# Latent attention's input projection: from plain fp32 matmuls to three products of rounded halves

## What is computed

```python
hx = rms_norm(x, norm_g[i]) * (1 + scx) + sx
hc = rms_norm(ctx, norm_g[i]) * (1 + scc) + sc
# mla_mixer(hc, hx, ...)
def project(h, rotate):
    cq, ckv, kr, gate = split_last(h @ w_in, (MLA_Q_RANK, MLA_KV_RANK, MLA_ROPE, MLA_WIDTH))  # 384, 256, 32, 1024
    q = (rms_norm(cq, q_norm_g) @ w_uq) ...
    kv = (rms_norm(ckv, kv_norm_g) @ w_ukv) ...
```

## Time and profile before

| | us |
|---|---|
| device time, median of 3 runs | 1794.86 (1794.18 to 1795.97) |
| the profiled execution, device time | 1794.53 |
| its span, first to last instruction | 1792.7 |
| PE busy in the span | 1705.8 (95%) |
| DVE busy | 1286.5 (72%) |
| ACT busy | 749.0 (42%) |

### The profile page before, as it was taken

How to read it: one execution, slowest core, us unless ns; L and a number is a source line. 1 busy time by engine, 2 the same in 40 slices (tenths; PEclk the granted TensorE clock), 3 DMA queues, 4 the chain that set the end, 5 groups by cost and what they waited for, 6 DMA issues and landing times. The chain is left out here.

```text
span 1792.7 us, 30064 instructions
## 1 busy us (share of the span) xinstructions
PE 1705.8 (95%) x12816; PEld 1491.0 (83%) x12816; DVE 1286.5 (72%) x1938; ACT 749.0 (42%) x974; POOL 6.3 (0%) x14
## 2 busy tenths in 40 slices
PE   2999989999999999998899999999999999999998
PEld 2999979877999989998898789999754556747898
DVE  7876887855877778997877567987552778566744
ACT  2433375333633373434652255342432445334354
POOL 0000000000000000000000000000000000000000
PEclk9999999999999999999999999999999999999999
DMA  9877536443577738883455336776152010251102
GB/s 390 346 280 281 209 118 225 144 187 118 207 289 273 313 118 338 315 308 120 157 209 193 137 141 253 279 279 227 61 203 84 1 47 1 109 231 48 48 25 94
DMA packets 48804, 331.87 MB, mean 185 GB/s; under 512 B 5256, under 2 KB 8480, under 8 KB 9376
## 3 DMA queue, kind: packets, MB, share of 16 engines
q1 hardware_dynamic: 47808, 326.79, 47.8%
q0 software_dynamic: 864, 3.17, 0.7%
HBM read 328.87 MB, written 1.07 MB: 184 GB/s over the span
## 5 line engine op out<-in xcount | busy, mean ns | idle before, releaser
L343 PE MATMUL ps<-xhi,low 128*128 128x256 f32 x2048 | 499.3, 283 | 4.4 <-ACT xhi L1407 4.2
L343 PEld LDWEIGHTS ps<-xhi,low 128*128 128x128 f32 x2048 | 360.5, 191 | 7.0 <-ACT xhi L1407 5.8
L343 PE MATMUL ps<-xhi,whi_wk 128*128 128x256 f32 x1072 | 298.0, 288 | 39.9 <-ACT xhi L1407 38.8
L343 PE MATMUL ps<-xlo,whi_wk 128*128 128x256 f32 x1072 | 290.7, 280 | 0.0
L1407 ACT ACTIVATE wk<-ps 128x256 f32<-128x256 f32 (+5 forms) x219 | 108.2, 502 | 432.5 <-PE ps L343 367.0
L343 PE MATMUL ps<-xa,ring 128*128 128x256 f32 (+1 forms) x1056 | 281.1, 424 | 5.2 <-DVE xa L1989 3.1
L1407 ACT ACTIVATE whi_wk<-ring 128x2048 fp32r<-128x2048 f32 x100 | 191.6, 1919 | 188.3 <-DMA ring<-in_stream_dram 138.1
L343 PEld LDWEIGHTS ps<-xa,ring 128*128 128x128 f32 x1056 | 197.6, 190 | 82.5 <-issue 51.4
L343 PEld LDWEIGHTS ps<-xhi,whi_wk 128*128 128x128 f32 x1072 | 202.8, 194 | 42.8 <-issue 41.2
L1986 DVE TENSOR_TENSOR low<-ring,whi_wk 128x2048 fp32r<-128x2048 f32 (+1 forms) x101 | 228.4, 2264 | 6.6 <-ACT whi_wk L1407 6.6
L343 PE MATMUL ps<-wk 64*64 64x64 f32 (+10 forms) x2712 | 210.3, 262 | 5.9 <-ACT wk L1407 4.3
(11 more groups left out here) (131 smaller groups left out, 2553.4 us busy)
## 6 DMA issues: line engine op xcount, KB each, us to landing
ring<-in_stream_dram SPq DMA_DIRECT2D x302, 1024.0 KB, 5.6
ring<-in_cond_dram SPq DMA_DIRECT2D x4, 1024.0 KB, 4.7
wk<-spread_dram POOLq DMA_DIRECT2D x4, 384.0 KB, 5.4
wk<-spread_dram POOLq DMA_DIRECT2D x2, 768.0 KB, 7.3
tab<-in_tab_dram SPq DMA_DIRECT2D x1, 1440.0 KB, 20.5
res<-in_xt_dram SPq DMA_DIRECT2D x1, 1024.0 KB, 17.5
res<-in_ct_dram SPq DMA_DIRECT2D x1, 1024.0 KB, 9.8
out_dram<-wk SPq DMA_DIRECT2D x4, 256.0 KB, 2.5
```

What stands on the lines that cost most here:

```text
L343: last[0] = nc.tensor.matmul(o, l, r, start=start, stop=stop, skip_group_check=free)
```

## The change

The seven `mla_in` chunks are taken with `take_both`, so that each has a high and a low half, made by ACT (`mla_high`) and DVE (`mla_low`): chunk 0 beside `w13` 20 of the feed-forward, chunks 1 and 2 at the head of `norm(5)`, chunk 3 after the third rank's copy, 4 between the two sums of the ranks, 5 and 6 after gate units 7 and 9. The modulated context and tokens go rounded into `whi_xa` (the memory of `xa`), and their low parts into `x2lo`, which needs the full value beside it: eight more ACT instructions for the context (`xf6`), eight more DVE instructions for the tokens (into `x2f`), and four subtractions on DVE. Each matmul over k becomes three in fp32r. For the context, units 0 to 3 run with the high half alone before `ms2`, 4 and 5 after it, and then all six get their third product. The late modulation chunks start only at chunk 2. `cq_sq` moves to column 4096, since `x2lo` takes its place, and the copy of the rotated key (`k_rope`) stands behind the first logarithm of the ranks.

```diff
+        x2lo = nc.alloc_sbuf_tensor_at("x2lo", [P, KT, 2 * T], F32R, offset=wk_at + 4 * NEW)
...
-        LATE_AT = (0, 1, 2, 3, 4, 5, 6)
+        LATE_AT = {2: (0,), 3: (1, 2), 4: (3, 4), 5: (5,)}
```

PE, in `mla`:

```diff
+                def input_halves(i):
+                    no = take_both("mla_in", i)
+                    eng.wait_ge(vector_done, step("mlow", i))
+                    return tiles(low[:, (no + 1) % RING, :], 256), tiles(low[:, no % RING, :], 256)
+                def with_high(n, both, cs):
+                    (hi, lo), at = both, slice(P * (n % 2), P * (n % 2) + P)
+                    o = bank(n % 6, cs.start, cs.stop)
                     for k in range(KT):
...
+                        if n == 0:
+                            eng.wait_ge(scalar_done, step("xc6" if cs == CS else "xx6", k))
+                        mm(o, hi[:, k, at], whi_xa[:, k, cs], k == 0, False, free=True)
+                        mm(o, lo[:, k, at], whi_xa[:, k, cs], False, False, free=True)
+                def with_low(n, both, cs):
+                    hi, at = both[0], slice(P * (n % 2), P * (n % 2) + P)
+                    for k in range(KT):
+                        if n == 0:
+                            eng.wait_ge(vector_done, step("xlc6" if cs == CS else "xlx6", k // 4))
+                        mm(bank(n % 6, cs.start, cs.stop), hi[:, k, at], x2lo[:, k, cs], False, k == KT - 1, free=True)
+                def unit(n, both):
+                    (hi, lo), at = both, slice(P * (n % 2), P * (n % 2) + P)
+                    for k in range(KT):
+                        mm(bank(n % 6), hi[:, k, at], whi_xa[:, k, :], k == 0, False)
+                        mm(bank(n % 6), lo[:, k, at], whi_xa[:, k, :], False, False)
+                        mm(bank(n % 6), hi[:, k, at], x2lo[:, k, :], False, k == KT - 1)
```

ACT, in `norm` and `mla` (and `mla_high(0)` in `ffn`):

```diff
+            def mla_high(i):
+                n = found["chunk_no", "mla_in", i][1]
+                eng.wait_ge(landed[n % RING], loads(n))
+                eng.wait_ge(*step_of("chunk", n + 1 - RING))
+                act(low[:, (n + 1) % RING, :], ring[:, n % RING, :], ACT.Copy, "mround", i).then_inc(scalar_done, 1)
...
                 if m == 5:
+                    mla_high(1)
+                    mla_high(2)
                     one_table()
...
+                    if m == 5 and kind == "w13" and j == 20:
+                        mla_high(0)
...
+                for t in range(KT):
+                    act(x3[:, t, CS], x3[:, t, CS], ACT.Identity, "xf6", t, scale=x[:, t, 1:2], bias=md[:, t, 1:2]).then_inc(scalar_done, 1)
                 eng.wait_ge(tensor_done, step("ms2", m))
...
+                    if n == 2:
+                        mla_high(3)
                 for i in range(2):
                     eng.wait_ge(tensor_done, step("cqsum", i))
                     log_mean(rs2[:, 512 * i:512 * i + 512], bank(6), (384, 256)[i], EPS, "cqe", i)
+                    if i == 0:
+                        mla_high(4)
+                        eng.wait_ge(vector_done, step("kr"))
+                        act(k_h[64:96, :, :], over(k_rot[64:96, :], 8), ACT.Copy, "k_rope").then_inc(scalar_done, 1)
                 root(rs2, "cqr", m)
                 for n in range(6, 14):
                     gate_out(n)
+                    if n in (7, 9):
+                        mla_high(5 + (n - 7) // 2)
```

DVE, in `norm` for m = 5 (ahead of the wait for `accb` 0), with `mla_low(0)` after `w13` 20 in `ffn`:

```diff
+                else:
+                    mla_low(1)
+                    mla_low(2)
```

DVE, in `mla`:

```diff
+                for i, hs in enumerate(halves):
+                    eng.wait_ge(scalar_done, step("xf6", 4 * i + 3))
+                    tt(x2lo[:, hs, CS], x3[:, hs, CS], whi_xa[:, hs, CS].bitcast(F32), SUB, "xlc6", i).then_inc(vector_done, 1)
                 eng.wait_ge(scalar_done, step("rs2", m))
                 for t in range(KT):
                     tt(x3[:, t, XS], res[:, t, XS], rs2[:, 256:512], MUL, "xn6", t).then_inc(vector_done, 1)
...
+                for t in range(KT):
+                    ts(x2f[:, t], x3[:, t, XS], x[:, t, 0:1], MUL, md[:, t, 0:1], ADD).then_inc(vector_done, 1)
...
+                for i, hs in enumerate(halves):
+                    eng.wait_ge(scalar_done, step("xx6", 4 * i + 3))
+                    tt(x2lo[:, hs, XS], x2f[:, hs], whi_xa[:, hs, XS].bitcast(F32), SUB, "xlx6", i).then_inc(vector_done, 1)
+                mod_part(*LATE_MODS[0])
+                mla_low(3)
                 eng.wait_ge(tensor_done, step("in2", m, 5))
...
+                mod_part(*LATE_MODS[1])
+                mla_low(4)
+                mod_part(*LATE_MODS[2])
                 eng.wait_ge(scalar_done, step("cqr", m))
...
+                mla_low(5)
+                mod_part(*LATE_MODS[3])
+                mla_low(6)
```

More of the change, by code:

```diff
@@ L857, in ada @@
                 def ada(i):
-                    if i == 0:
+                    if i == 2:
                         leave("cond2", 2)
-                    for c in range(LATE_AT[i], LATE_AT[i + 1]):
+                    for c in LATE_AT[i]:
                         leave("ada", *LATE_MODS[c])
@@ L973, in mla @@
                 for i in range(3):
-                    w = tiles(take("mla_in", i), 256)
-                    early.append((w, held[0]))
-                    ada(i)
+                    both = input_halves(i)
+                    early.append((both, held[0]))
                     if i == 2:
+                        ada(i)
                         eng.wait_ge(scalar_done, step("ve", 5))
                     for n in (2 * i, 2 * i + 1):
-                        unit(n, w, CS)
-                    if i == 0:
+                        with_high(n, both, CS)
+                    if i == 1:
                         for t in range(KT):
@@ L986, in mla @@
                         done.named("ms2", m)
+                for n in range(6):
+                    with_low(n, early[n // 2][0], CS)
                 for i in range(3):
[L988 to L992, removed]
+                    both, held[0] = early[i]
+                    pair = (2 * i, 2 * i + 1)
+                    for n in pair:
+                        with_high(n, both, XS)
+                    for n in pair:
+                        with_low(n, both, XS)
                         ended(n)
@@ L1010, in mla @@
                             eng.wait_ge(*step_of("in2_read", m, n - 6))
-                        unit(n, w, slice(0, 512))
+                        unit(n, both)
                         held[0] = mine
@@ L1713, in mla @@
                     eng.wait_ge(vector_done, step("xn6", t))
-                    act(xa[:, t, XS], x3[:, t, XS], ACT.Identity, "xx6", t, scale=x[:, t, 0:1], bias=md[:, t, 0:1]).then_inc(scalar_done, 1)
+                    act(whi_xa[:, t, XS], x3[:, t, XS], ACT.Identity, "xx6", t, scale=x[:, t, 0:1], bias=md[:, t, 0:1]).then_inc(scalar_done, 1)
                 conditions(2)
@@ L1760, in mla @@
                     found["in2_read", m, n] = found["cqsq", n]
-                eng.wait_ge(vector_done, step("kr"))
-                act(k_h[64:96, :, :], over(k_rot[64:96, :], 8), ACT.Copy, "k_rope").then_inc(scalar_done, 1)
+                    if n == 2:
+                        mla_high(3)
                 for i in range(2):
@@ L2061, in win_low, with mla_low @@
                 tt(low[:, n % RING, :], ring[:, n % RING, :], low[:, (n + 1) % RING, :].bitcast(F32), SUB, "wlow", m, i).then_inc(vector_done, 1)
+            def mla_low(i):
+                n = found["chunk_no", "mla_in", i][1]
+                eng.wait_ge(scalar_done, step("mround", i))
+                tt(low[:, n % RING, :], ring[:, n % RING, :], low[:, (n + 1) % RING, :].bitcast(F32), SUB, "mlow", i).then_inc(vector_done, 1)
             def lows(m, c, part=None):
@@ L2193, in ffn @@
                         gate(m)
+                    if m == 5 and kind == "w13" and j == 20:
+                        mla_low(0)
                     if m == 5 and kind == "w13" and j == 18:
@@ L2447, in mla @@
                     tt(x3[:, t, XS], res[:, t, XS], rs2[:, 256:512], MUL, "xn6", t).then_inc(vector_done, 1)
-                for c in range(2):
-                    mod_part(*LATE_MODS[c])
+                eng.wait_ge(vector_done, done.count)
+                for t in range(KT):
+                    ts(x2f[:, t], x3[:, t, XS], x[:, t, 0:1], MUL, md[:, t, 0:1], ADD).then_inc(vector_done, 1)
+                eng.wait_ge(vector_done, done.count)
+                for i, hs in enumerate(halves):
[3 more added lines that the diff above has]
+                mla_low(3)
                 eng.wait_ge(tensor_done, step("in2", m, 5))
```

17 lines of the change are left out of this document (6 added, 11 removed).

## The result

| | before | after |
|---|---|---|
| median of 4 runs each, us | 1794.52 (1793.86 to 1795.97) | 1782.7 (1781.35 to 1784.08) |
| the profiled execution, us | 1794.53 | 1784.08 |
| its span, us | 1792.7 | 1782.2 |

The ratio is 0.9933, with a 95% interval of 0.9916 to 0.995. The change makes the kernel 11.8 us faster. The forecast was 16.4 us faster and 1778.4 us, with a range that ended at 1782.0. So the direction and the mechanism were right, the size was not, and the measured time lies 0.7 us outside the range.

A forecast was written before the change was run, and what follows sets the result against it. PE's steps alone were taken to bound the projection. 10.2 us from units of 512 columns plus 6.3 from those of 256 made 16.5, taken as 16.4: median from 1794.9 to 1778.4 us, range 1776.0 to 1782.0.

The forecast's parts named there:

- what bounds: In the projection PE's steps alone set the end; DVE and ACT have 69 and 77 us to spare.
- The eight units of 512 columns: In the projection, each unit gets 1.27 us cheaper, 10.2 us in all, if the halves come in time.
- the price of a step: fp32r steps in the projection cost 0.118 us at 256 columns and 0.233 us at 512, as in existing fp32r rows.
- Loads in the open: Rival: in the projection every third weight load of 0.188 us lies open, +13.7 us, 1808 us in all; chance 3%.
- the covers: Halves ready before PE wants them: 1.1 us ahead of `accb`, 3 us or more for tokens, 2 us at chunk 5.
- The low halves of chunks 1 and 2: In `norm(5)`, DVE finishes them at 1248.05, 1.1 us before `accb` at 1249.19; cost nothing, at most 1 us.
- Chunk 3: Projection weights, released 1289.8, usable 1299.9 after ACT copies rank 2, wanted 1303.7.
- `xlx6`: Low parts of the tokens, done by DVE at 1284.4 and wanted by PE at 1287.9; costs nothing.
- Chunk 5: Projection weights, released 1316.6, usable 1325.7, wanted 1327.8; the tightest cover, with 2 us.
- Unit 0 gains nothing, since ACT paces it: The context's first unit follows ACT's `xc6` hand-overs, gains nothing and owes its third product, 0.94 us.
- The 6.3 us for the units of 256 columns: Context units: `cqsum` 0 starts at 1301.1 instead of 1307.4, 6.3 us earlier.
- the four: Rivals: loads in the open 3%, late halves (1780.5 to 1783.5) 9%, faster steps (1775) 3%, given back in heads (1790) 1%.

The follow-up runs named there:

- `paced_fill`: Changed kernel plus two unread fp32r matmuls beside each of the eight high-product pairs of the context's unit 0: 1780.5 us, ratio 0.9916 to before.
- `pair`: Changed kernel with the high products of the context's units 0 and 1 both advancing at each ACT hand-over: 1778.84 us, ratio 0.9907 to before.
- `two_products`: Changed kernel without the third product (high half times `x2lo`) throughout the projection, halves still made and awaited: 1767.87 us, ratio 0.9834 to before.
- `before_again`: The kernel before, unchanged, run again for a second profile: 1796.96 us, ratio 1.0004 to before.
- `before_look2`: The kernel before, unchanged, one more single profiled execution: 1795.96 us.
- `after_look1`: The changed kernel, unchanged, one more single profiled execution: 1784.75 us.
- `gla_fill`: Changed kernel plus three unread matmuls with ones in PE's wait at the start of the next mixer: 1782.18 us, ratio 0.9924 to before.
- `after_again`: The changed kernel, unchanged, run again for a second profile: 1784.16 us, ratio 0.9934 to before.
- `pair_gla`: Changed kernel with both the paired first two context units and the three filling matmuls at the next mixer's start: 1778.07 us, ratio 0.9903 to before.
- `before_sparse`: The kernel before with the context's unit 0 multiplied over only half of its 256 rows: 1798.76 us, ratio 1.0019 to before.

## Why the prediction was right and wrong

**Right: what bounds.** PE's steps alone set the end of the projection, and the gain came out of them. The eight units of 512 columns with what stands between them (`cqsum` 0 to T1) took 74.12 us and take 63.71 (1306.01 to 1369.72): 10.41 us less, 10.2 forecast.

**Right: the price of a step**, 0.118 and 0.232 us in the new place (0.118 and 0.233 forecast). The rival *Loads in the open* is refuted in the place itself. The weight loads of the third products, 160 of them, 187 to 193 ns long by this row of after:

```profile
L345 PEld LDWEIGHTS ps<-x2lo,low x160: 187/188/193, 1283.1 to 1362.1; 128*128 128x128 f32 x160
```

Where 48 such loads and steps follow one another, a step takes 0.118 us. The Trainium skill (TensorE: Matmul & The Clock Gate, the section The mechanism) says that a load overlaps matmuls in flight only when it is for another row group; with full 128 x 128 loads that does not hold here. The same section also lets a load for the background weight buffer be pulled ahead, which would fit; no run here shows which buffer a load goes to. The gap that the same page of the Trainium skill (Back-to-back issue gap) gives for an isolated matmul of 512 columns, 216 ns, is 16 ns under the step measured here.

**Right: the covers.** Each named cover held, most within about a microsecond. Timeline of DVE in after, the answer to the earlier trace rows:

```profile
1245.94 4.49 DVE L2032 TENSOR_TENSOR low<-ring,low 128x2048 fp32r<-128x2048 f32 x2 [0.16 <-ACT low L1434]
1251.75 0.88 DVE L2038 SCALAR_TENSOR_TENSOR wk<-ps,aux,wk 128x256 f32<-128x256 f32 x2 [1.32 <-PE ps L345]
...
1302.47 2.29 DVE L2032 TENSOR_TENSOR low<-ring,low 128x2048 fp32r<-128x2048 f32 x1 [8.89 <-ACT low L1434]
...
1328.34 2.29 DVE L2032 TENSOR_TENSOR low<-ring,low 128x2048 fp32r<-128x2048 f32 x1 [4.07 <-ACT low L1434]
```

The low halves of chunks 1 and 2 end 1.32 us before `accb` (1.1 forecast). Chunk 3 is usable at 1304.76 and wanted at 1308.19. `xlx6` ends at 1288.41 and its first step, the row at 1292.70, is 4.3 us behind it. Chunk 5 is the tightest, as forecast: its first step, the one behind the 72 of units 7 to 9, starts at 1332.55, and it is usable at 1330.63, so 1.9 us are left (2 forecast). Its rounding on ACT, with chunk 4's, answers to the earlier trace rows:

```profile
1311.64 1.92 ACT L1434 ACTIVATE low<-ring 128x2048 fp32r<-128x2048 f32 x1 [2.17 <-DMA ring<-in_stream_dram]
...
1326.39 1.92 ACT L1434 ACTIVATE low<-ring 128x2048 fp32r<-128x2048 f32 x1 [3.69 <-DMA ring<-in_stream_dram]
```

**Wrong: the sentence "Unit 0 gains nothing, since ACT paces it".** It is true of unit 0's own end and was taken as the end of the matter. The 6.3 us for the units of 256 columns rest on it and on the clock of 1.00 that the earlier trace rows show for before. But the change halves what PE does in just that stretch, and the granted clock is not a property of the stretch; here it followed from what PE does in it. Measured from T0 to `cqsum` 0, before has 53.74 us and after 49.78: 3.96 instead of 6.3. In `paced_fill` it is 48.20 (1253.87 to 1302.07) less the open 0.24, that is 5.78. So of the 2.3 us that this term missed, 1.8 are the clock. The other 0.5 are where unit 0's products end (0.1) and what follows them: from unit 1's first step to `cqsum` 0 `paced_fill` needs 35.85 us (1266.22 to 1302.07), and 35.45 were forecast. No rival had the clock in it; of the four, none describes what happened.

**Wrong: the width.** I gave 1 us to each side for the steps and 1 for the median, and nothing for falls that differ between executions of the same code. Behind T1 they cost after 1.3 us. Ahead of T0 the profiled executions differ by 2.57 us in code that the change leaves alone but for chunk 0's halves beside `w13` 20 and two chunks' halves behind it. Windows of before, then of after:

```profile
234.00:238.00 4.00, 4.00 (x30) 3.74 (x31) 3.93 (x12) 4.00 (x6) 0.00 (x0) 1.00 0.00 0
388.00:394.00 6.00, 6.00 (x50) 4.62 (x49) 4.14 (x8) 0.80 (x2) 0.00 (x0) 1.00 0.01 3
```

```profile
234.00:238.00 4.00, 4.00 (x19) 3.82 (x19) 3.92 (x12) 3.99 (x6) 0.00 (x0) 0.57 0.01 4
388.00:394.00 6.00, 6.00 (x32) 5.00 (x32) 1.67 (x5) 0.80 (x2) 0.00 (x0) 0.51 0.01 3
```

The same work at the two clocks, long before the changed code. T0 lies between 1253.66 and 1255.17 in the four executions of before, and between 1255.36 and 1256.23 in the three of after; `paced_fill`, `pair` and `two_products`, which have the same code up to T0 as after, start it at 1253.87, 1253.62 and 1256.32. So T0 differs by up to 2.7 us with the execution, and the profiled before was an early one. It goes with the falls: `before`, `paced_fill` and `pair` have none at 42, 234 or 388 us and lie within 0.25 us of each other; with a fall at 42 us alone `before_again` and `before_look2` have 1255.17 and 1255.09, `after_look1` and `gla_fill` 1255.36 and 1255.45. At equal falls the changed code ahead of T0 thus costs 0.4 us at most. The falls at 234 and 388 us together stand in four of the nine executions with the change (`after`, `after_again`, `pair_gla`, `two_products`) and in none of the five without it; whether the change has a part in that is not settled.

**The sum, again.** 16.4 forecast; less 2.0 in the stage (1.8 of it the clock), less 1.3 behind T1, less 2.57 ahead of T0 gives the 10.5 us of the profiled pair. The median's gain is 11.8: the stage's 14.4 less 1.3 is 13.1, and the remaining 1.3 us may be falls elsewhere in executions that were not profiled; that part is not shown.

## What to carry to other kernels

Where a change makes PE's work cheaper, look for the stretches in which PE is paced by another engine: it gains nothing there in time, and with less work in them its clock may fall and take the first microseconds behind them too. Fill such a stretch with work that is due anyway, by advancing two units with each hand-over, before thinking of dummies. And the granted clock in a row of before holds for the work of before only.

## What the runs showed of the hardware

- A fall of the granted clock from 2.4 to 1.2 GHz can follow from a change that removes matmul work without a longer way for what it waits for: with 0.24 instead of 0.43 us of matmuls in each hand-over of some 0.5 us it fell in all five profiled executions of after, `gla_fill` and `two_products`, and in `before_sparse`, which does half of before's work there. The falls read at the stretches above lasted 3.4 or 6.8 us, and one of 6.8 us cost 1.8 us in the end, since part of it lay in waiting (an estimate from the stages of after and `paced_fill`).
- At equal work, a fall may come in one execution and not in another (the windows at 234 and 388 us), and the time ahead of T0 goes with it, by as much as 2.7 us.
- Behind a wait of PE of about 3 us the clock fell in both places where `two_products` made one, which adds up to 1.7 us to the wait. The 3.14 us wait at the next mixer's start had the fall in eight executions and not in the four of before.
